# Cross attention scores as three passes of rounded parts instead of one full-precision pass

## The reference

```python
h2 = rms_norm(x, norm2_g[l])
m = rms_norm(mem, norm_mem_g[l])
qa = (h2 @ xa_wq[l]).reshape(B, L, XA_HEADS, XA_DH)
ka = (m @ xa_wk[l]).reshape(B, M, XA_HEADS, XA_DH)
va = (m @ xa_wv[l]).reshape(B, M, XA_HEADS, XA_DH)
s = jnp.einsum('blhd,bmhd->bhlm', qa, ka).astype(jnp.float32) * XA_DH ** -0.5
p = jax.nn.softmax(s, axis=-1).astype(va.dtype)
o = jnp.einsum('bhlm,bmhd->blhd', p, va).reshape(B, L, XA_HEADS * XA_DH)
x = x + o @ xa_wo[l]
```

## Time and profile before

| | us |
|---|---|
| median of 3 runs | 2441.59 (2440.62 to 2441.76) |
| the profiled execution | 2440.76 |
| its span, first to last instruction | 2438.9 |
| attention stage, first scores to first matmul of `xo` | 1037.30 to 1093.64 |

### The profile page before, as it was taken

One profiled execution on the slowest core, in us unless ns is written; L12 is line 12 of the kernel. 1 busy time (PEld: TensorE's weight loads), 2 busy tenths in 40 slices (PEclk: granted clock), 3 DMA queues, 4 the chain that ended last, 5 costly groups with the idle time before them and its releaser, 6 DMA issues.

```text
span 2438.9 us, 35222 instructions
## 1 busy us (share of the span) xinstructions
PE 2373.0 (97%) x14746; PEld 1975.6 (81%) x14746; DVE 1450.8 (59%) x2462; ACT 678.0 (28%) x1095; POOL 194.1 (8%) x89
## 2 busy tenths in 40 slices
PE   7999999999999999999999999889999999999998
PEld 6788888887878888988887887777888878888887
DVE  5785259927996241471623543664666657777777
ACT  3211112124221031151423426441344432121123
POOL 1001000000000240202000000001000000000000
PEclk9999999999999999999999999999999999999999
DMA  7345653255576516332053352122245555434442
GB/s 233 125 138 184 210 173 104 95 178 184 175 228 216 208 61 216 134 108 104 22 211 110 122 162 76 55 76 105 63 163 203 191 198 199 146 126 138 138 146 88
DMA packets 269201, 354.30 MB, mean 145 GB/s; under 512 B 34961, under 2 KB 159858, under 8 KB 269042
## 3 DMA queue, kind: packets, MB, share of 16 engines
q1 hardware_dynamic: 236066, 301.56, 37.8%
q10 hardware_dynamic: 32976, 50.48, 5.6%
HBM read 244.93 MB, written 107.05 MB: 144 GB/s over the span
## 4 chain that ended last, share of the span: by engine, by line
PE 80%; DVE 9%; DMA 4%; issue 3%; ACT 3%; SPq 1%; ACTq 0%; DVEq 0%
PE PS L518 27%; PE PS L521 16%; PE PS L3384 15%; PE PS L3464 9%; PE PS L1969 1%; PE PS L697 1%; DVE W_LO L416 1%; PE PS L1985 1%; PE PS L2594 1%; DMA x_d<-X 1%; PE PS L1322 1%; PE PS L2589 1%; PE PS L1185 1%; PE PS L1318 1%; DMA CB<-pch_d 1%
## 5 line engine op out<-in xcount | busy, mean ns | idle before, releaser
L518 PE MATMUL PS<-W_HI,OP_HI 128*128 128x512 f32 (+1 forms) x1152 | 294.9, 399 | 7.6 <-POOL W_HI L451 5.8
L518 PE MATMUL PS<-W_LO,OP_HI 128*128 128x512 f32 (+1 forms) x1152 | 280.8, 386 | 0.7 <-DVE W_LO L416 0.7
L518 PE MATMUL PS<-W_HI,OP_LO 128*128 128x512 f32 (+1 forms) x1152 | 279.1, 384 | 0.0
L451 POOL TENSOR_SCALAR W_HI<-RAW 128x2048 fp32r<-128x2048 f32 (+1 forms) x66 | 133.0, 2027 | 1510.6 <-PE PS L518 668.5
L518 PEld LDWEIGHTS PS<-W_HI,OP_HI 128*128 128x128 f32 x1152 | 209.8, 191 | 52.1 <-POOL W_HI L451 6.2
L518 PEld LDWEIGHTS PS<-W_LO,OP_HI 128*128 128x128 f32 x1152 | 214.3, 189 | 45.2 <-DVE W_LO L416 1.0
L518 PEld LDWEIGHTS PS<-W_HI,OP_LO 128*128 128x128 f32 x1152 | 212.5, 188 | 42.7 <-issue 0.5
L547 ACT ACTIVATE OST<-PS 128x512 f32<-128x512 f32 (+2 forms) x152 | 85.7, 564 | 443.9 <-PE PS L521 244.2
L416 DVE TENSOR_TENSOR W_LO<-RAW,W_HI 128x2048 fp32r<-128x2048 f32 (+1 forms) x58 | 138.8, 2410 | 78.2 <-POOL W_HI L451 58.7
L521 PE MATMUL PS<-OP_HI,W_HI 128*128 128x512 f32 x704 | 179.1, 396 | 0.0
L521 PE MATMUL PS<-OP_HI,W_LO 128*128 128x512 f32 x704 | 174.2, 389 | 0.0
(11 more groups left out here) (528 smaller groups left out, 3719.0 us busy)
## 6 DMA issues: line engine op xcount, KB each, us to landing
RAW<-in_w_gate_up SPq DMA_DIRECT2D x88, 512.0 KB, 5.9
RAW<-in_w_in SPq DMA_DIRECT2D x28, 1024.0 KB, 7.1
RAW<-in_w_out SPq DMA_DIRECT2D x12, 1024.0 KB, 8.4
LE<-spill_d SPq DMA_DIRECT2D x22, 512.0 KB, 4.1
RAWD<-in_w_down SPq DMA_DIRECT2D x11, 1024.0 KB, 5.1
X<-x_d SPq DMA_DIRECT2D x4, 2048.0 KB, 8.9
x_d<-X SPq DMA_DIRECT2D x2, 4096.0 KB, 18.3
ptok_d<-OST ACTq DMA_DIRECT2D x24, 256.0 KB, 2.0
```

The lines of the kernel that those rows point to most:

```text
L451: nc.gpsimd.tensor_scalar(hi, raw, 1.0, 1.0, ALU.mult, ALU.mult).then_inc(*w_hi.by(1))
L518: ins = nc.tensor.matmul(PS[:, bank, 0:width], act_part[:, k, a * P:(a + 1) * P], w_part[:, slot, k, 0:width], start=start, stop=stop)
```

## The change

The scores are computed like a projection. A query tile is split by two new steps: ScalarE copies `QTL` rounded to the tile's columns of `OP_HI` (`act_query_hi`), and VectorE writes `QTL` minus that to `OP_LO` (`dve_query_lo`). Tile 0 and the high part of tile 1 are split while the values are projected (`act_first_query`, `dve_first_query`); the low parts of tiles 1 and 2 stand in front of VectorE's loop, and those of tiles 3 to 7 behind `greatest` in a round. Keys are split where values are: ScalarE writes `KH`, VectorE the low part to `KLa` or `KLb` (`dve_memory_keys`), and only the second step frees the bank. A tile's scores are 24 matmuls of 128x256 in the rounded type. They wait for the low part of their tile instead of the tile's load, and a load of queries waits for a low part instead of scores. `KLa` takes the place of `GROWF`, whose load moves behind that of x1. Two new steps count on semaphores of the stage (`xa_e`, `xa_nm`, `xv_hi`), so their totals and the waits on them change. In the diff the tables of totals, the waits that only count differently and the calls that add the new generators to their stages are left out.

```diff
@@ -336,7 +336,7 @@
     add_gemm("out_s5", w_out, cols(0, D), "tok", TT, row0=D, engine="dve")
     add_gemm("out_ret", w_out, cols(0, D), "tok", TT, row0=0, engine="dve")
     add_gemm("xq", I["xa_wq"][0], cols(0, D), "ch", L, half_first=True)
-    add_gemm("xk", I["xa_wk"][0], cols(0, D), "ch", MEM)
+    add_gemm("xk", I["xa_wk"][0], cols(0, D), "ch", MEM, engine="dve")
     add_gemm("xv", I["xa_wv"][0], cols(0, D), "ch", MEM, engine="dve")
     for name in ("xk", "xv"):
...
-    KA = at("KA", "extra", 7168, [P, KT, MEM])
+    KH = at("KH", "extra", 7168, [P, KT, MEM], F32R)
+    KL2 = (at("KLa", "extra", 0, [P, KT - 1, MEM], F32R), at("KLb", "small", 1024, [P, 1, MEM], F32R))
...
             if t >= 2:
-                sp.wait_ge(*xa_s(t - 1))
+                sp.wait_ge(*query_lo_done(t - 2))
...
-            act.activation(KA[:, 4 * (b - g.first_block) + a, :], PS[:, unit_bank[g.first + n], 0:width], ACT.Copy)\
-               .then_inc(*bank_act.by(1))
+            act.activation(KH[:, 4 * (b - g.first_block) + a, :], PS[:, unit_bank[g.first + n], 0:width], ACT.Copy)\
+               .then_inc(*xv_hi.by(1))
+
+    def key_low(k):
+        return KL2[k // (KT - 1)][:, k % (KT - 1), :]
+
+    def dve_memory_keys(dve):
+        g = gemms["xk"]
+        for n, (b, a, _, width) in enumerate(g.units):
+            yield n + 1.0
+            dve.wait_ge(*xv_hi(n + 1))
+            k = 4 * (b - g.first_block) + a
+            nc.vector.tensor_tensor(key_low(k), PS[:, unit_bank[g.first + n], 0:width], KH[:, k, :].bitcast(F32),
+                                    ALU.subtract).then_inc(*bank_dve.by(1))
+
+    def exps_done(t):
+        return xa_e(min(5 * t + 6, 5 * TT))
+
+    def query_hi_done(t):
+        return xa_e(5 * t - 3 if t else 1)
+
+    def query_lo_done(t):
+        return xa_nm(2 * t + 1)
+
+    def act_query_hi(act, t):
+        if t == 0:
+            act.wait_ge(*mm_done(gemms["xq"].end))
+        act.wait_ge(*xa_q[t % 2](16 * (t // 2 + 1)))
+        act.activation(OP_HI[:, :, t * P:(t + 1) * P], QTL[:, t % 2], ACT.Copy).then_inc(*xa_e.by(1))
+
+    def dve_query_lo(dve, t):
+        dve.wait_ge(*query_hi_done(t))
+        nc.vector.tensor_tensor(OP_LO[:, :, t * P:(t + 1) * P], QTL[:, t % 2],
+                                OP_HI[:, :, t * P:(t + 1) * P].bitcast(F32), ALU.subtract).then_inc(*xa_nm.by(1))
+
+    def act_first_query(act):
+        yield XV_START + 0.3
+        act_query_hi(act, 0)
+        yield XV_START + 2.2
+        act_query_hi(act, 1)
+
+    def dve_first_query(dve):
+        yield XV_START + 0.7
+        dve_query_lo(dve, 0)
...
         def scores(t):
-            pe.wait_ge(*xa_q[t % 2](16 * (t // 2 + 1)))
+            pe.wait_ge(*query_lo_done(t))
             if t >= 2:
-                pe.wait_ge(*xa_e(4 * (t - 1)))
+                pe.wait_ge(*exps_done(t - 2))
+            tokens = slice(t * P, (t + 1) * P)
             for h in range(XH):
-                for k in range(2):
-                    ins = T.matmul(PS[:, 2 * (t % 2) + h // 2, (h % 2) * MEM:(h % 2 + 1) * MEM],
-                                   QTL[:, t % 2, 2 * h + k, :], KA[:, 2 * h + k, :], start=k == 0, stop=k == 1)
+                place = PS[:, 2 * (t % 2) + h // 2, (h % 2) * MEM:(h % 2 + 1) * MEM]
+                for i in range(3):
+                    for k in (2 * h, 2 * h + 1):
+                        ins = T.matmul(place, (OP_LO if i == 2 else OP_HI)[:, k, tokens],
+                                       key_low(k) if i == 1 else KH[:, k, :],
+                                       start=i == 0 and k == 2 * h, stop=i == 2 and k == 2 * h + 1)
             ins.then_inc(*xa_s.by(1))
...
         probabilities(0)
         for t in range(TT):
+            if t + 2 < TT:
+                act_query_hi(act, t + 2)
...
         greatest(0)
+        dve_query_lo(dve, 1)
         greatest(1)
+        dve_query_lo(dve, 2)
         shares(0)
         for t in range(TT):
             if t + 1 < TT:
...
             if t + 2 < TT:
                 greatest(t + 2)
+            if t + 3 < TT:
+                dve_query_lo(dve, t + 3)
             yield t
...
                      sp_retention(sp), sp_retention_stores(sp), sp_s5_operand(sp), sp_ret_operand(sp),
                      sp_s5_sum_loads(sp), sp_s5_sum_stores(sp), sp_x_halves(sp))
-            sp_gain(sp, 3)
             sp.wait_ge(*rt_out(16 * TT))
...
             sp_weights(sp, weights_before("xo"))
             sp.wait_ge(*xa_lo(TT))
             sp.dma_start(X[:, :, :], rows_of(x1_d)).then_inc(*x_in.by(16))
+            sp_gain(sp, 3)
             sp_weights(sp, weights_before("pa"))
```

More of the change, by code:

```diff
@@ L69 @@
 for later, earlier, total in (e.split() for e in (
-        "gm r_turn 8, dec r_sc 8, tr r_o 8, la r_kv 7, c1 xw_lo 8, ex r_qkt 8, rt r_root 8, trc xv_hi 8, e1 r_trig 2,"
+        "gm r_turn 8, dec r_sc 8, tr r_o 8, la r_kv 7, c1 xw_lo 8, ex r_qkt 8, rt r_root 8, trc xv_hi 16, e1 r_trig 2,"
         "ag r_scr 8, ss r_var 8, kk r_on 8, s r_rst 8, lt r_g 8, ct r_ang 1, in0 rq_in 128, in1 rv_in 128, v0 glu_z 16,"
@@ L75 @@
 for later, earlier, total in (e.split() for e in (
-        "sg_w xa_s 8, sg_mm xa_t 8, sg_t xw_mm 8, sg_gl xw_hi 8, sg_root xa_hi 8, sg_hi xa_e 32, sg_wt xa_nm 8,"
+        "sg_w xa_s 8, sg_mm xa_t 8, sg_t xw_mm 8, sg_gl xw_hi 8, sg_root xa_hi 8, sg_hi xa_e 40, sg_wt xa_nm 16,"
         "sg_var xa_p 8, sg_vn xa_lo 8, sg_y r_ab 16, sg_lo r_rot 8, su_in0 xa_q0 64, su_in1 xa_q1 64, xw_lo r_back 8, xv_hi r_hi 8").split(",")):
@@ L1945, in dve_memory_values @@
             yield n + 1.0
-            dve.wait_ge(*xv_hi(n + 1))
+            dve.wait_ge(*xv_hi(len(g.units) + n + 1))
             k = 4 * (b - g.first_block) + a
@@ L1976, in values @@
             if n == TT - 1:
-                pe.wait_ge(*xa_e(4 * TT))
+                pe.wait_ge(*exps_done(TT - 1))
             elif n:
@@ L1987, in values @@
             ins.then_inc(*xw_mm.by(1))
-        pe.wait_ge(*bank_act(gemms["xk"].free1_act))
+        pe.wait_ge(*bank_dve(gemms["xk"].free1_dve))
         pe.wait_ge(*bank_dve(g.free0_dve + 6))
@@ L2017, in probabilities @@
         def probabilities(t):
-            act.wait_ge(*xa_nm(t + 1))
+            act.wait_ge(*xa_nm(2 * t + 2))
             if t >= 2:
@@ L2050, in shares @@
             st_ = XST[:, t % 2]
-            dve.wait_ge(*xa_e(4 * (t + 1)))
+            dve.wait_ge(*exps_done(t))
             chain(V.reciprocal(st_[:, 3, :], st_[:, 2, :]))
@@ L3874, in _ @@
                      later(2 * TT, act_gemm_store_steps(act, "xq", ch_to(qa_d))), act_memory(act),
-                     paced(act_memory_keys(act), XK_START, XK_UNIT), paced(act_memory_values(act), XV_START, XK_UNIT))
+                     paced(act_memory_keys(act), XK_START, XK_UNIT), paced(act_memory_values(act), XV_START, XK_UNIT),
+                     act_first_query(act))
             act_attention(act)
@@ L3904, in _ @@
                      dve_split_later(dve, "xk", (24.6, 25.15, 32.6, 33.0)), dve_split_later(dve, "xv", (34.9, 35.3, 36.95, 37.35)),
[L3905 removed]
+                     paced(dve_memory_keys(dve), XK_START, XK_UNIT), paced(dve_memory_values(dve), XV_START, XK_UNIT), dve_first_query(dve), dve_split_later(dve, "xo", (39.3, 39.8)))
             together(dve_attention(dve, chain), dve_split_later(dve, "xo", (0.1, 1.1), skip=2))
@@ L3938, in _ @@
             pe_attention(pe)
-            together(one_after_other(pe_gemm_steps(pe, "xo", ready=[(xa_e, 4 * TT)], operand=(xa_lo, 0), folded=xw_lo), 2 * TT,
+            together(one_after_other(pe_gemm_steps(pe, "xo", ready=[(xa_e, 5 * TT)], operand=(xa_lo, 0), folded=xw_lo), 2 * TT,
                                      pe_gemm_steps(pe, "pa", operand=(op_lo_done, turned_base(4)))),
```

## The result

The changed kernel takes 2451.21 us (median of 8 runs, 2444.97 to 2454.11), the kernel before 2440.78 on the same chip (8 runs). The two medians differ by 10.4 us. The estimated ratio of the two kernels' times is 1.0034, with a 95% interval of 1.0023 to 1.0045, which is 8.3 us (5.6 to 11.0) where 5.6 were forecast. The median itself lies 1.0 us above the forecast's range; the forecast's base of 2441.59 times the ratio gives 2449.9, inside the range, near its upper end. The mechanism was the forecast one. The start of the stage cost almost twice its term, and two of the rivals came true beside it: the clock, and a late x1 for another reason than the one given.

A forecast was written before the change was run, and what follows sets the result against it. The prediction took two nearly equal chains, TensorE's and VectorE's, to bound the attention stage, with VectorE's lengthening paid in full. Start 3.3 plus rounds 2.3 made 5.6 us, on 2441.59 giving 2447.2 us; range 2443.4 to 2450.2.

The forecast's parts named there:

- the forecast's base of 2441.59: Time of the kernel before: median of the runs shown, 0.8 us above the profiled execution's 2440.76.
- The mechanism: Attention stage: TensorE and VectorE chains nearly equally long; shortening TensorE's gains next to nothing, lengthening VectorE's is paid in full.
- The start of the stage: First scores to largest score 2: scores 1 wait for tile 1's low part on VectorE; 3.3 us lost, 1.0 of it GpSimd.
- the clock: Rival, start of stage: TensorE's idle stretch drops its clock to 1.2 GHz, 1.7 us more lost; 2448.9 us, chance 0.17.
- a late x1: Rival, in `xo`: gain row queued behind x1 shares its queues and delays it, 1.3 us more; 2448.5 us, chance 0.08.
- The rival that TensorE's shorter scores decide: Attention stage: VectorE's new work hides completely, eight tiles each save 0.39 us; gain 3.1 us, 2438.5 us, chance 0.06.
- a stall in the middle of `xo`: Sign listed as showing the forecast wrong; no size given.
- Rounds: Five rounds, largest score 2 to 7: new low part costs 1.14 us in each of two with a weight split; 2.3 us.
- The cover in the other rounds: Three rounds without a split: the 1.14 us low part fits VectorE's 2.00 us wait for exponentials, no cost, 0.86 left.
- GpSimd's exclusion: Start of stage: GpSimd's W_HI split of `xo` blocks VectorE's low part of tile 1; 1.0 us of the start's loss.
- The rest at nothing: Outside start and rounds: key low parts fall into VectorE's waits, removed gain-row load lay beside other work; no cost.

The follow-up runs named there:

- all_before2: Changed kernel with all eight query tiles split before the stage, tiles 4 to 7 behind the third, fourth, seventh and eighth key units; ratio to the kernel before 1.0001.
- pool_later: Changed kernel with GpSimd's last rounding of half a weight block of `xo` held until tile 1's low part is made; ratio to the kernel before 1.0012.
- gain_late: Changed kernel with SyncE waiting until x1 has landed before it issues the gain row's load; ratio to the kernel before 1.0024.
- filler50: Changed kernel with 50 unread matmuls of 128x160 in TensorE's wait between scores 0 and scores 1; ratio to the kernel before 1.0033.
- the control: The changed kernel run once more, unaltered; ratio to the kernel before 1.0031.
- low1_early: Changed kernel with the low part of query tile 1 made by VectorE during the value projection; ratio to the kernel before 1.0025.

## Why the prediction was right, and where it was short

**Direction and place: right.** The loss lies in the attention stage, at the start and in the two rounds with a split, and it goes when the low parts leave the stage (all_before2). The rival that TensorE's shorter scores decide is refuted by the same comparison: the matmuls did get shorter (2.95 a tile, 2.88 as forecast, against 3.27), and the rounds gained nothing from it (35.41 against 35.48) until VectorE's chain was cut (34.65). One of the prediction's own signs against it did appear, a stall in the middle of `xo`; it comes with the late x1 below.

**Rounds: 2.3 forecast, 2.21 measured.** The cover in the other rounds held: 2.00 us of waiting became 0.87.

**The start: 3.3 forecast, 6.04 measured.** This term was mis-sized. Its steps without GpSimd give 16.8 us from first scores to largest score 2 (17.8 as forecast, less the 1.0), and pool_later, which has just these steps, took 16.87. GpSimd's exclusion took 1.33 instead of 1.0, and it stopped the negation ahead of the low part, not the low part itself. The rest, 2.4, is the clock: I had it as a rival at 0.17 and 1.7 us, since only one fall was shown and the values might have taken the blow instead. The clock was already falling within the wait, so scores 1, the first work behind it, took it whole, 5.26 us against 2.95. A forecast that itself announces the longest wait of the stage should have carried the clock in its sum.

**x1: the size nearly right, the reason wrong.** Counted as a rival at 0.08 and 1.3 us; TensorE lost 0.93. That the size came near is luck: not the gain row (gain_late) but a packet of program code in the load goes with the delay, and more TensorE instructions ahead of `xo` moved it out (filler50). That the change's own added matmuls had moved it in is likely, but no run shows it alone.

**The rest at nothing: held.** TensorE shows no wait in keys and values; ScalarE's copies took 1.05 to 1.09 each, without cost but for that of tile 2, which shows once the low part of tile 1 is out of the way. With the measured terms the sum is 6.04 + 2.21 + 0.93 = 9.2, and 2450.8 on the forecast's base, 0.6 above its range: two rivals of the forecast, each priced alone, came together.

## What to carry to other kernels

Price a new step by where it stands in the order of the engine that others wait for: two subtractions of 1.2 us ahead of waits cost 6 us here (with the GpSimd pass and the clock), two in rounds without slack 1.1 each, three in slacks nothing. A wait that the forecast gives to TensorE can be charged twice, once as time and once as the clock of the work behind it: here 1.3 us less of it gave back 3.7. An edit in TensorE's code can also move the loads of program code behind it, so a stall far from the edit need not come from the work that the edit adds.

## What the hardware showed unasked

A VectorE instruction on 128x4 elements of one tensor waits for a GpSimd pass too: 1.51 and 1.58 us instead of 0.17, until GpSimd's 1.90 us were over. The kernel before already had it, smaller, against the GpSimd pass that ends at 1042.48; the forecast looked only at the low part:

```profile
1042.21 0.29 DVE L2047 TENSOR_SCALAR XST<-XST 128x4 f32<-128x4 f32 x1
```

The Trainium skill ("SBUF — State Buffer", Who interferes with whom) describes an exclusive lock on a shared port pair; these waits agree with it, for a step with one small input tensor.

Falls of the granted clock come and go between executions of one kernel: in the control's profile the clock was 0.50 from 686 to 690, in the changed kernel's own it was 1.00 there (windows of the two):

```profile
686.00:690.00 4.00, 3.00 (x18) 2.62 (x19) 2.14 (x3) 0.94 (x2) 0.00 (x0) 0.50 1.01 303
```

```profile
686.00:690.00 4.00, 4.00 (x23) 3.37 (x22) 3.96 (x4) 1.65 (x3) 2.55 (x2) 1.00 0.15 55
```

Single runs of one kernel differ by up to 10.7 us (before: 2437.15 to 2447.88 in 23 runs), and the time goes with the clock: the fastest of these runs has a mean granted clock of 0.996, the slowest 0.992, and 0.004 of the span is 9.8 us. So a stretch of the trace settles here what the total cannot. Why the first 4.07 us of waiting let the clock fall and 2.74 did not, while 2.83 did in low1_early, stays open.
